# Forget-gate attention pairs with outputs by feature, reciprocals turned with the weights, and scores in 64-row halves

## What is computed

```python
proj = h @ w_in
fq, fk, fv, fgate, dq, dk, dv = jnp.split(proj, IN_SPLITS, axis=-1)
log_f = jax.nn.log_sigmoid(fgate + fox_forget_b)
c = jnp.cumsum(log_f, axis=1).transpose(0, 2, 1)
fox_o = causal_block_attention(fq, fk, fv, c)     # per head, blocks of 128 queries:
#   s = q @ k.T * 0.125 + c[t] - c[s], masked above the diagonal
#   out = softmax(s) @ v
return concatenate([fox_o, diff_o], axis=-1) @ w_out
```

## Time and profile before

| | |
|---|---|
| time, median of 3 runs | 995.57 us (992.7 to 996.19) |
| span of the profiled execution | 990.5 us |
| instructions | 14542 |
| TensorE matmul busy | 986.0 us, 5302 instructions |
| VectorE busy | 711.5 us, 849 instructions |
| ScalarE busy | 486.3 us, 621 instructions |
| GpSimd busy | 213.1 us, 215 instructions |
| mean granted TensorE clock | 1.000 |
| fox pairs and the whole w_out product | about 269 to 314 us of the span |

### The profile page before, as it was taken

One profiled execution on the slowest core, in us unless ns is written; L12 is line 12 of the kernel. 1 busy time (PEld: TensorE's weight loads), 2 busy tenths in 40 slices (PEclk: granted clock), 3 DMA queues, 4 the chain that ended last, 5 costly groups with the idle time before them and its releaser, 6 DMA issues.

```text
span 990.5 us, 14542 instructions
## 1 busy us (share of the span) xinstructions
PE 986.0 (100%) x5302; PEld 835.5 (84%) x5302; DVE 711.5 (72%) x849; ACT 486.3 (49%) x621; POOL 213.1 (22%) x215
## 2 busy tenths in 40 slices
PE   9999999999999999999999999999999999999998
PEld 6888888888888888888888888888888888888887
DVE  6766666775788767676777998678875767667674
ACT  6534343664666543434545444365555445334342
POOL 3313232014100232323112600060000012223230
PEclk9999999999999999999999999999999999999999
DMA  9665656745425656565745625544536456556561
GB/s 316 224 212 169 212 169 214 253 131 190 129 85 170 209 173 210 171 205 177 247 154 174 204 94 200 188 145 147 168 121 220 130 184 230 172 178 201 179 210 42
DMA packets 121017, 178.53 MB, mean 180 GB/s; under 512 B 5760, under 2 KB 82112, under 8 KB 120848
## 3 DMA queue, kind: packets, MB, share of 16 engines
q1 hardware_dynamic: 120048, 174.86, 53.8%
q0 software_dynamic: 576, 1.39, 0.5%
q10 hardware_dynamic: 352, 1.73, 0.5%
HBM read 176.88 MB, written 2.64 MB: 181 GB/s over the span
## 4 chain that ended last, share of the span: by engine, by line
PE 99%; DMA 0%; SPq 0%; ACT 0%; issue 0%; DVE 0%
PE acc L662 11%; PE acc L666 10%; PE acc L665 10%; PE tp L863 10%; PE gu L863 10%; PE gu L868 5%; PE tp L868 5%; PE tp L662 4%; PE tp L666 4%; PE tp L665 4%; PE gu L662 3%; PE gu L665 3%; PE gu L666 3%; PE acc L1143 2%; PE acc L1146 1%; PE acc L1172 1%
## 5 line engine op out<-in xcount | busy, mean ns | idle before, releaser
L2002 DVE TENSOR_TENSOR wlo<-raw,whi 128x2048 fp32r<-128x2048 f32 x140 | 325.7, 2331 | 153.9 <-ACT whi L1363 152.4
L1363 ACT ACTIVATE whi<-raw 128x2048 fp32r<-128x2048 f32 x150 | 285.7, 1908 | 70.3 <-PE acc L666 22.7
L863 PE MATMUL tp<-act_in,whi 128*128 128x512 f32 x432 | 102.9, 390 | 0.0
L863 PE MATMUL gu<-act_in,whi 128*128 128x512 f32 x432 | 102.6, 390 | 0.0
L1899 POOL TENSOR_TENSOR tmp<-tmp 128x256 f32<-128x256 f32 x54 | 39.7, 736 | 275.8 <-DVE tmp L2123 275.8
L1901 POOL TENSOR_TENSOR sil<-sil,tmp 128x256 f32<-128x256 f32 x54 | 88.8, 1644 | 33.5 <-ACT sil L1434 33.5
L863 PEld LDWEIGHTS gu<-act_in,whi 128*128 128x128 f32 x432 | 80.9, 188 | 16.6
L662 PE MATMUL acc<-whi,hT_hi 128*128 128x512 f32 x240 | 94.0, 392 | 0.0
L665 PE MATMUL acc<-wlo,hT_hi 128*128 128x512 f32 x240 | 93.7, 390 | 0.0
L666 PE MATMUL acc<-whi,hT_lo 128*128 128x512 f32 x240 | 93.4, 389 | 0.0
L863 PEld LDWEIGHTS tp<-act_in,whi 128*128 128x128 f32 x432 | 79.8, 188 | 15.7
(11 more groups left out here) (379 smaller groups left out, 1845.8 us busy)
## 6 DMA issues: line engine op xcount, KB each, us to landing
raw<-in_w_in SPq DMA_DIRECT2D x96, 512.0 KB, 4.7
raw<-in_down SPq DMA_DIRECT2D x66, 512.0 KB, 4.1
raw<-in_gate SPq DMA_DIRECT2D x64, 512.0 KB, 4.4
raw<-in_up SPq DMA_DIRECT2D x64, 512.0 KB, 4.9
raw<-in_w_out SPq DMA_DIRECT2D x16, 512.0 KB, 4.7
raw<-in_w_branch_hg SPq DMA_DIRECT2D x8, 512.0 KB, 4.3
raw<-in_w_branch_attn SPq DMA_DIRECT2D x8, 512.0 KB, 4.8
post<-in_post_gains SPq DMA_DIRECT2D x3, 512.0 KB, 6.2
```

Of the source, the lines that this page charges most:

```text
L863: pe.matmul(banks[:, a, :], w_hi[:, i, a * P:(a + 1) * P], both, start=i == 0, stop=False)
L1363: act.activation(split_weights(k)[0], raw[:, k % RING, :], ACT.Copy).then_inc(hi_ready, 1)
L2002: dve.tensor_tensor(w_lo, raw[:, k % RING, :], w_hi.bitcast(F32), ALU.subtract).then_inc(lo_ready, 1)
```

## The change

1. **Scores (pairs 4 to 7).** Queries and keys of both heads stay where the transposes put them, head 0 on rows 0 to 63, head 1 on rows 64 to 127, copied by one operation each instead of two. The score matmuls are 64-row ones, the two heads' results in two banks, as for the differential pairs. The decays are no longer rows of these operands but separate bf16 matmuls of 6 rows: each decay is split into three bf16 parts, by five small GpSimd operations before the DMA. The memsets of GpSimd at L1905 and L1906 and of VectorE at L2505 and L2506 give way to two on GpSimd.
2. **Values.** v is loaded as weights (128 rows, 64 columns), and the turned weights are streamed, so that the output has features on partitions: head 0 on 0 to 63, head 1 on 64 to 127 (column tiles).
3. **Scaling.** The sums now belong to columns. VectorE takes the reciprocals of the sums spread over 64 columns each (128x256, `fox_reciprocals`) right behind the exps; TensorE turns them with two more transposes in `turn_weights`; the copies to `fox_pT` take them along (512 columns each); one VectorE multiply makes the scaled output (128x256, in `dec_sb`), ScalarE rounds it straight into `act_hi` (`fox_hi`), VectorE puts the rest in `act_lo` (`fox_lo`).
4. **w_out.** Fills 2 and 3 go. The fox half of the product waits for `fox_lo` of three pairs, its last tile for the fourth.
5. **Order.** On VectorE `fox_reciprocals(p)` stands ahead of a half of a low part and ahead of the copy of the pair's weights; the split maxima of pairs 5 and 6 become whole ones, ahead of `k_out`. TensorE waits for both copies of the weights before values in pairs 6 and 7 too.

```diff
-AUG = 64 + 2
+AUG = 6
-                if kind == 1:
+                if kind < 2:
                     at = [slice(64 * h, 64 * h + 64) for h in range(2)]
+                    q, k = (fox_q[:, i, :], fox_k[:, i, :]) if kind == 0 else (q_sb[:, 0, :], k_sb[:, 0, :])
...
+                    if kind == 0:
+                        decay = [slice(64 * h, 64 * h + AUG) for h in range(2)]
+                        for h in range(2):
+                            pe.matmul(late_half(p, h), aug_q[decay[h], i, P:S], aug_k[decay[h], i, :], start=False,
+                                      stop=False, skip_group_check=True)
+                        for h in range(2):
+                            pe.matmul(early_half(p, h), aug_q[decay[h], i, 0:P], aug_k[decay[h], i, 0:P], start=False,
+                                      stop=False, skip_group_check=True)
@@ turn_weights
+                if pair(p)[0] == 0:
+                    pe.wait_ge(exp_done, p + 1)
+                    for h in range(2):
+                        for n in range(3):
+                            to = (n + 1) % 3 * P
+                            pe.transpose(turned[:, h, to:to + P], e_sb[:, h, n * P:(n + 1) * P], idn)
+                    pe.wait_ge(rden_ready, p + 1)
+                    for t in range(TT):
+                        mm = pe.transpose(turned[:, t, 3 * P:4 * P], fox_rden(p)[:, (1 - t) * P:(2 - t) * P], idn)
                     mm.then_inc(pT_full, 1)
@@ values
+                if kind == 0:
+                    at = [slice(64 * h, 64 * h + 64) for h in range(2)]
+                    v = [proj[:, t, FV + i * P:FV + (i + 1) * P] for t in range(TT)]
+                    o = fox_place(p)
+                    for h in range(2):
+                        pe.matmul(o[at[h], 0, :], v[0][:, at[h]], fox_pT[:, h, 0:P], start=True, stop=True,
+                                  skip_group_check=True)
+                    for h in range(2):
+                        pe.matmul(o[at[h], 1, :], v[0][:, at[h]], fox_pT[:, h, P:S], start=True, stop=False,
+                                  skip_group_check=True)
+                    for h in range(2):
+                        mm = pe.matmul(o[at[h], 1, :], v[1][:, at[h]], fox_pT[:, h, S:3 * P], start=False, stop=True,
+                                       skip_group_check=True)
@@ after the pairs, TensorE
-            pe.wait_ge(o_out, 8)
-            fills(T_WOUT, from_proj(MIX), 2, 3)
             half(N_WOUT + 1, 0, wout_banks(1), 1, 1, first_j=1)
-            filled(T_WOUT, 3)
...
+            pe.wait_ge(fox_lo_ready, 3)
+            half(N_WOUT + 2, 0, wout_banks(0), 0, 0, tiles=[0, 1, 2], first_j=1)
+            pe.wait_ge(fox_lo_ready, 4)
+            half(N_WOUT + 2, 0, wout_banks(0), 0, 0, tiles=[3], first_j=1).then_inc(acc_bank, 1)
@@ ScalarE
+            def fox_hi(p):
+                act.wait_ge(o_out, p + 1)
+                act.activation(heads(act_hi[:, p - 4, :], 2), fox_scaled(p), ACT.Copy).then_inc(fox_hi_ready, 1)
@@ ScalarE, loop over pairs 4 to 7
+                    else:
+                        hi(N_WOUT + 3)
                     if p == 4:
                         next_hi(N_WIN, 0, 23)
+                    fox_hi(p)
@@ VectorE
+            def fox_reciprocals(p):
                 dve.wait_ge(exp_done, p + 1)
-                dve.reciprocal(rden[:, n:n + 4], den[:, :]).then_inc(rden_ready, 1)
+                dve.reciprocal(heads(fox_rden(p), 4), per(den[:, :], 64)).then_inc(rden_ready, 1)
+            def fox_lo(p):
+                dve.wait_ge(fox_hi_ready, p - 3)
+                dve.tensor_tensor(heads(act_lo[:, p - 4, :], 2), fox_scaled(p), heads(act_hi[:, p - 4, :].bitcast(F32), 2),
+                                  ALU.subtract).then_inc(fox_lo_ready, 1)
@@ output
+                if kind == 0:
+                    dve.wait_ge(pv_done, p + 1)
+                    dve.wait_ge(pT_a, p + 1)
+                    dve.tensor_tensor(fox_scaled(p), fox_place(p), fox_pT[:, :, 3 * P:4 * P], ALU.mult).then_inc(o_out, 1)
+                    return
@@ order on VectorE
                 fill_scaled(T_WOUT, 1)
+                fox_reciprocals(4)
                 half_lo(N_WOUT, 1)
                 block_out(N_WIN, 0, 23)
                 fill_rest(T_WOUT, 0)
                 weights_out(4)
-                late_maxima(5)
+                maxima(5)
                 k_out(6)
-                maxima(5, late_found=True)
                 output(4)
                 fill_rest(T_WOUT, 1)
+                fox_reciprocals(5)
                 half_lo(N_WOUT + 1, 0)
                 weights_out(5)
-                late_maxima(6)
+                maxima(6)
                 k_out(7)
-                maxima(6, late_found=True)
                 output(5)
+                fox_lo(4)
+                fox_reciprocals(6)
                 half_lo(N_WOUT + 1, 1)
-                reciprocals(6)
                 maxima(7)
                 weights_out(6)
                 output(6)
+                fox_lo(5)
+                fox_reciprocals(7)
                 half_lo(N_WOUT + 2, 0)
                 weights_out(7)
+                fox_lo(6)
+                output(7)
                 half_lo(N_WOUT + 2, 1)
-                output(7)
+                fox_lo(7)
```

More of the change, by code:

```diff
@@ L62 @@
 BY_TILE, BY_HALF = [(0, 0), (0, 1), (1, 0), (1, 1)], [(0, 0), (1, 0), (0, 1), (1, 1)]
-DIFF_FIRST = [(0, 1), (1, 1), (0, 0), (1, 0)]
-FILLS = [DIFF_FIRST if u == T_WOUT else BY_HALF if u in (T_FFN1, T_WOUT2) else BY_TILE for u in range(9)]
+DIFF_ONLY = [(0, 1), (1, 1)]
+FILLS = [DIFF_ONLY if u == T_WOUT else BY_HALF if u in (T_FFN1, T_WOUT2) else BY_TILE for u in range(9)]
 C_ID, C_TRI, C_ONES, C_MASK, C_COS, C_SIN, C_SAME = 0, 128, 256, 384, 512, 528, 544
@@ L984, in scores @@
                 for h in range(2):
[L985 to L997, removed]
+                    q, k = q_sb[:, h, :], k_sb[:, h, :]
+                    pe.matmul(late_half(p, h), q[:, P:S], k, start=True, stop=True)
+                    mm = pe.matmul(early_half(p, h), q[:, 0:P], k[:, 0:P], start=True, stop=True)
                 mm.then_inc(scores_done, 1)
@@ L1015, in turn_weights @@
                     mm.then_inc(pT_full, 1)
[L1016 to L1021, removed]
             def values(p):
@@ L1547, in weights_out @@
                     act.wait_ge(pv_done, p)
-                n = S if pair(p)[0] == 1 else 3 * P
-                act.activation(pT_sb[:, 0, 0:n], turned[:, 0, 0:n], ACT.Copy).then_inc(pT_a, 1)
+                n = (4 * P, S, 3 * P)[pair(p)[0]]
+                to = pT_sb if pair(p)[0] else fox_pT
+                act.activation(to[:, 0, 0:n], turned[:, 0, 0:n], ACT.Copy).then_inc(pT_a, 1)
             def diff_and_fox():
@@ L1725, in _ @@
             diff_and_fox()
-            hi(N_WOUT + 3)
-            fills(T_WOUT, 2, 3)
             hi(N_FFN2)
@@ L2211, in k_out, with maxima @@
                        .then_inc(kT_ready, 1)
-            def late_maxima(p):
-                dve.wait_ge(scores_done, p + 1)
-                n = 4 * (p % 2)
-                dve.tensor_reduce(mx[:, n:n + 2], heads(late(p), 2), AX, ALU.max)
-            def maxima(p, late_found=False):
+            def maxima(p):
                 dve.wait_ge(scores_done, p + 1)
@@ L2250, in weights_out @@
                     return
-                dve.tensor_copy(pT_sb[:, 1, :], turned[:, 1, 0:3 * P]).then_inc(pT_d, 1)
-                if pair(p)[0] == 0 and p != 6:
-                    reciprocals(p)
+                to, n = (pT_sb, 3 * P) if pair(p)[0] else (fox_pT, 4 * P)
+                dve.tensor_copy(to[:, 1, 0:n], turned[:, 1, 0:n]).then_inc(pT_d, 1)
             def late_reciprocals(p):
```

117 lines of the change are left out of this document (57 added, 60 removed).

## The result

The changed kernel takes 996.27 us (median of 9 runs, 995.64 to 999.27), the kernel before beside it 992.87 us (9 runs, 992.59 to 996.19): ratio 1.0027, 95% interval 1.0014 to 1.0040. So it is slower by about 3.4 us. The forecast was 999.9 us and +4.3. The profiled execution of before is of the lower level, that of after of the upper: its span is 996.6 us, and TensorE reaches the scores of pair 4 at 272.19 us.

What follows compares the result with a forecast made beforehand. TensorE was taken to bound the kernel before, VectorE's chain pairs 4 to 7 after: values(7) +5.2 us, less 0.87 us of fills, gives +4.3; 995.57 + 4.3 = 999.9 us, own range 998.3 to 1001.5, wider 993.4 to 1002.6.

Steps and rivals of the forecast that it cites:

- rival B: VectorE's wide reciprocal is cheap, 0.3 to 0.4 us, so TensorE's saving stays: 993.9 us; chance 0.18.
- the base: Whole kernel before: profiled span 990.5 us plus 5.07 us to the median of three timed runs, 995.57 us.
- The price of the reciprocal: VectorE, pairs 4 to 7: a 128x256 reciprocal takes 2.27 us, 2.19 from start to start.
- VectorE's chain sets the pace: Pairs 4 to 7: with four reciprocals VectorE decides; values(7) ends at 302.01 instead of 296.82 us, +5.2 us.
- the fill's rest: Behind pair 4's reciprocal: TensorE comes at about 278.0 us and gets the fill's rest 1.6 us later.
- the turning in pair 5: TensorE idles 0.75 us before turning the next queries and keys, behind VectorE's work for pair 5.
- values(6): TensorE idles 1.9 us for VectorE's copy of pair 6's weights, ready at 295.22 us.
- pair 7's turned reciprocals: TensorE idles 1.9 us at the two transposes of pair 7, whose reciprocal ends the chain at 299.30 us.
- After 302 us nothing new waits: Behind values(7): fox lo(7) is ready before its first read, and the x halves come about 1 us early.
- TensorE's work: Per pair scores -0.07, turning +0.22, values -0.39 us; fills 2 and 3 save 0.87 once; sum -1.8 us.
- Rival C: Slow reciprocals and no overlap of the array's halves: scores 1.9, values 1.46 us; +6.1 us, 1001.7 us; chance 0.07.
- rival D: TensorE's clock falls after the idle before pair 7, costing 1.6 to 3.2 us: 1002.3 us; chance 0.05.

Runs made afterwards that it cites:

- e4: The changed kernel with single reciprocals of several widths, plain or spread, behind its last VectorE instruction; 6.25 ns per column over a base of about 153 ns.
- e2: The changed kernel with the half low part of w_out piece 2 moved directly behind the copy of pair 7's weights; 996.24 us, ratio to before 1.0012.
- e8: The kernel before with four more 128x256 reciprocals on VectorE, unread and waiting for nothing, at the change's places; 997.24 us, ratio 1.0044.
- e6: e3 with the products of values in the old form (weights stationary, 64 columns of values streamed); 996.13 us, 1.8 us over e3 at the lower level.
- e3: The changed kernel with reciprocals of four columns spread by a copy, and the half low part moved as in e2; 992.03 us, ratio to before 0.9982.
- e5: The changed kernel with the half low part moved as in e2 and every 128x256 reciprocal issued twice; 1005.3 us.
- e9: The kernel before with nine instead of seven matmuls on zeroes at its start; 992.5 us.
- e10: The changed kernel with nine instead of seven matmuls on zeroes at its start; 995.79 us.
- e7: e3 with nine instead of seven matmuls on zeroes at the start of TensorE's program; 991.9 us, ratio to before 0.9978.

## Why the prediction was right and wrong

The time came out 3.6 us under the forecast of 999.9. The step that put it outside the range of 998.3 to 1001.5 (it lies within the wider 993.4 to 1002.6, which reaches into rival B) is the base of 995.57 us, 2.7 us too high; the cost of a wide reciprocal, 2.19 us where 1.66 was measured, is the largest error in the change itself.

**The price of the reciprocal: right kind, wrong size.** The step "4 elements take 168 ns, 8 take 203 ns, which is 8.75 ns for each further element" took a slope over four columns from two rows with different operands and stretched it over 248. In e4, where all widths have the same operands, the 4-wide one takes 178 ns and the 8-wide one 203: 6.25 ns per column instead of the 8.5 that the sum went on with, and 248 x 2.25 ns = 0.56 us less. A difference of 10 ns between two short rows was carried over 248 columns. The kind (iterative, far from 0.42 us) was right, and rival B with its cheap reciprocal is out; the 1.75 us lie inside the bounds 0.42 to 2.3. The Trainium skill ("VectorE: DVE Perf Modes", the walkthrough of the 8-slice pipeline) gives Reciprocal a repeat count of 8. The trace agrees that it is several times dearer per column than a tensor_tensor (0.43 us at the same width), and gives 6.25 ns.

**VectorE's chain sets the pace: right.** Four waits came at the places named: the fill's rest (0.76 for 1.6), the turning in pair 5 (0.23 for 0.75), values(6) (1.40 for 1.9), pair 7's turned reciprocals (0.95 for 1.9); together 3.3 us where 6.8 were forecast. Those predicted ahead of the transposes of pairs 5 and 6 (0.3 and 0.4) did not. The end of values(7) came 2.65 us later than before instead of 5.2. Four reciprocals of 0.53 us less are 2.1 us; this covers most of the difference, and with the real 1.66 the same walk gives about +2.2 us for the whole stretch without the x wait. e2, which has no x wait, shows 39.69 - 37.85 = +1.84, and e8 the pace alone, +4.48 for 4.4.

**"After 302 us nothing new waits": wrong.** I walked TensorE's readers of each low part, but not the queue of SP, which waits for the low part that the change moved behind output(7). Of a step that is moved, its release of a slot counts as well: the half low part starts at 303.13 instead of 295.43 us, 4.5 us later once the 3.20 us are taken out, the DMA of 5.6 us starts behind it, and what was to come "about 1 us before they are read" came 0.99 us late. e2 shows this cause alone: 1.12 us of the stretch.

**TensorE's work: right.** Scores 1.35 us and 0.10 to get in, 1.45 as predicted, the bf16 matmuls at their overlapped price. Turning eight blocks takes 0.80 us, +0.22 as said. Values take 0.81 us and 0.10 to get in, where 0.87 was said for all of it; e6 gives 0.34 us saved in pairs 4 and 5 for 0.39. e3 keeps 1.07 us of the 1.8, with 0.75 us of waits left for VectorE's and ScalarE's copies. Rival C is out.

**The clock: right here, near in e5.** It stayed at 1.00 in the changed kernel, so rival D did not happen; e5 shows it as a real one.

**The base: wrong by one level, and this is what put the time outside the range.** "5.07 us more" between span and time is two things: 1.8 us in every run (996.6 and 998.46 us in the profiled one after), and 3 us of the level that the median of three happened to have. So the span of 990.5 us, of the lower level, was set against a time of the upper one. The nine runs of the kernel before have the median 992.87, which with +4.3 would have given 997.2. So 999.9 us was above by 3.6: the base puts 2.7 of it, and 4.3 instead of 3.4 the rest. The two errors in the change itself (2.2 too much for the reciprocals, 1.1 missing for x) partly cancel, which is why +4.3 looks closer than its steps were. The stretch accounts for 2.3 to 3.0 us of the +3.3 to +3.4. The profiled executions leave next to nothing outside it (of 2.5 us between the spans of e9 and e10, 2.3 lie in the stretch); what the medians have more is what the executions of one kernel differ by.

## What to carry to other kernels

When an instruction moves in an engine's order, follow everything that it releases, the slots of the DMA queue too: here 1.2 us of VectorE work behind the wrong neighbour cost as much through a late transfer. An engine that is 80% busy beside the bound one is not free: four reciprocals of 1.66 us more became 4.5 us, with no new dependence. Compute on few values and spread afterwards: a reciprocal of four columns and a copy (0.18 + 0.29 us) in place of 256 reciprocals (1.75 us) turned this change from a loss of 3.4 us into a gain with e2's move.

## What the runs showed of the hardware

A reciprocal in fp32 on VectorE takes about 153 ns and 6.25 ns per column, 1.75 us at 128x256, whether its input is spread by a stride of zero or not, while a copy that spreads four columns to 256 takes 0.29 us. TensorE can run at half pace for some 7 us at the start although the profile's row of the granted clock says 1.00 there; only the distance between starts (0.43 against 0.23 us) shows it. Windows of the changed kernel at the start, with the clock of 1.00 and 13 matmuls in 4 us where the next four have 21:

```profile
8.00:12.00 4.00, 4.00 (x13) 2.93 (x12) 1.97 (x8) 2.18 (x8) 0.00 (x0) 1.00 1.08 361
12.00:16.00 4.00, 4.00 (x21) 3.24 (x20) 3.49 (x7) 2.90 (x5) 2.19 (x3) 1.00 1.08 355
```

Two matmuls more on zeroes ahead of the first input removed that phase, 3 us, from all 12 runs of e7, on a chip where about half of the runs had it.
